# The last expert of a layer: its context rounds, its two scatters and where their row numbers come from

## What is computed

```python
def ec_moe(h, w_router, w_gate, w_up, w_down):
    cap = EC_CAPACITY * length // N_EXPERTS
    aff = jax.nn.softmax((h @ w_router).astype(jnp.float32), axis=-1)
    g, idx = lax.top_k(jnp.swapaxes(aff, 1, 2), cap)
    xg = jax.vmap(lambda hb, ib: hb[ib])(h, idx)
    hid = jax.nn.silu(jnp.einsum('becd,edf->becf', xg, w_gate)) * jnp.einsum('becd,edf->becf', xg, w_up)
    out = jnp.einsum('becf,efd->becd', hid, w_down) * g.astype(h.dtype)[..., None]
    return jax.vmap(lambda ib, ob: jnp.zeros((length, dim), ob.dtype).at[ib.reshape(-1)].add(ob.reshape(-1, dim)))(idx, out)
...
x_lat = x_lat + mod[5] * ec_moe(h_lat, ...)
if not last:
    x_ctx = x_ctx + mod_c[5] * ec_moe(h_ctx, ...)
```

## Time and profile before

| | |
|---|---|
| time, median of three runs | 2590.0 us (2586.6 to 2592.71) |
| span of the profiled execution | 2588.7 us |
| TensorE busy | 2371.9 us (92%) |
| VectorE busy | 1783.0 us (69%) |
| ScalarE busy | 1378.9 us (53%) |
| GpSimd busy | 204.1 us (8%) |
| experts of layer 0, from the first gather to the last scatter's landing | 746.5 to 1529.6 us |
| experts of layer 1, likewise | 1978.7 to 2563.9 us |

### The profile page before, as it was taken

One profiled execution on the slowest core, in us unless ns is written; L12 is line 12 of the kernel. 1 busy time (PEld: TensorE's weight loads), 2 busy tenths in 40 slices (PEclk: granted clock), 3 DMA queues, 4 the chain that ended last, 5 costly groups with the idle time before them and its releaser, 6 DMA issues.

```text
span 2588.7 us, 34812 instructions
## 1 busy us (share of the span) xinstructions
PE 2371.9 (92%) x13396; PEld 1831.0 (71%) x13396; DVE 1783.0 (69%) x1997; ACT 1378.9 (53%) x1410; POOL 204.1 (8%) x220
## 2 busy tenths in 40 slices
PE   6999999989849999999999969988984999999994
PEld 4887777678636666666666647876864788888883
DVE  6523213455587888888888767566658899999995
ACT  6310113334525666656666644657353777777774
POOL 0000000000010211111111010000000011111110
PEclk9999999999879999999999988999997999999997
DMA  6034545735316887887887851112355999999995
GB/s 246 25 105 133 166 143 124 291 116 212 139 51 259 292 302 291 292 303 282 297 307 277 308 176 29 29 37 77 123 183 190 351 377 398 390 388 387 387 378 187
DMA packets 194343, 585.58 MB, mean 226 GB/s; under 512 B 19656, under 2 KB 64448, under 8 KB 187712
## 3 DMA queue, kind: packets, MB, share of 16 engines
q1 hardware_dynamic: 178688, 529.61, 54.9%
q0 software_dynamic: 12336, 48.24, 7.2%
q10 hardware_dynamic: 3216, 6.29, 0.7%
HBM read 536.88 MB, written 47.21 MB: 226 GB/s over the span
## 4 chain that ended last, share of the span: by engine, by line
PE 85%; DVE 6%; DMA 4%; ACT 4%; issue 1%; SPq 0%; POOL 0%; POOLq 0%; ACTq 0%; DVEq 0%
PE ps L1662 14%; PE ps L1664 13%; PE ps L1663 13%; PE ps L1677 7%; PE ps L578 5%; PE ps L579 4%; PE ps L580 4%; PE ps L849 3%; PE ps L850 3%; PE ps L851 3%; PE ps L515 1%; PE ps L549 1%; PE ps L615 1%; DMA R_W<-in_ada_w 1%; PE ps L617 1%
## 5 line engine op out<-in xcount | busy, mean ns | idle before, releaser
L1888 DVE TENSOR_TENSOR R_H_r<-R_M,R_W_r 128x2048 fp32r<-128x2048 f32 x336 | 759.0, 2287 | 141.0 <-ACT R_W_r L1790 138.6
L1790 ACT CAST R_W_r<-R_M 128x2048 fp32r<-128x2048 f32 x336 | 640.0, 1915 | 214.9 <-PE ps L1664 213.6
L1664 PE MATMUL ps<-R_W_r,R_C_r 128*128 128x512 f32 x1536 | 606.0, 395 | 0.0
L1662 PE MATMUL ps<-R_W_r,bc_r 128*128 128x512 f32 x1024 | 411.6, 402 | 5.8 <-ACT R_W_r L1790 2.9
L1663 PE MATMUL ps<-R_H_r,bc_r 128*128 128x512 f32 x1024 | 403.3, 394 | 0.0
L1664 PEld LDWEIGHTS ps<-R_W_r,R_C_r 128*128 128x128 f32 x1536 | 288.6, 188 | 65.6
L1662 PEld LDWEIGHTS ps<-R_W_r,bc_r 128*128 128x128 f32 x1024 | 192.5, 188 | 65.3 <-issue 10.9
L578 PE MATMUL ps<-R_H_r,R_W_r 128*128 128x512 f32 (+1 forms) x632 | 232.7, 368 | 4.9 <-ACT R_W L2251 2.0
L579 PE MATMUL ps<-R_C_r,R_W_r 128*128 128x512 f32 (+1 forms) x632 | 229.4, 363 | 0.0
L580 PE MATMUL ps<-R_H_r,R_W_r 128*128 128x512 f32 (+1 forms) x632 | 228.9, 362 | 0.0
L1663 PEld LDWEIGHTS ps<-R_H_r,bc_r 128*128 128x128 f32 x1024 | 192.5, 188 | 42.2
(11 more groups left out here) (323 smaller groups left out, 3766.3 us busy)
## 6 DMA issues: line engine op xcount, KB each, us to landing
R_M<-in_moe_w_gate SPq DMA_DIRECT2D x114, 1024.0 KB, 8.3
R_M<-in_moe_w_down SPq DMA_DIRECT2D x112, 1024.0 KB, 9.3
R_M<-in_moe_w_up SPq DMA_DIRECT2D x110, 1024.0 KB, 7.8
bc<-in_ada_w SPq DMA_DIRECT2D x28, 1024.0 KB, 4.9
R_H<-in_moe_w_up SPq DMA_DIRECT2D x18, 1024.0 KB
R_H<-in_moe_w_down SPq DMA_DIRECT2D x16, 1024.0 KB
R_H<-in_moe_w_gate SPq DMA_DIRECT2D x14, 1024.0 KB
R_W<-in_ev_w_in SPq DMA_DIRECT2D x25, 512.0 KB, 3.9
```

Source lines behind the costliest of these rows:

```text
L1662: pe.matmul(o, hi[:, k, :], wh[:, kk, cs], start=(k == 0), stop=False)
L1664: ins = pe.matmul(o, lo[:, k, 0:P], wh[:, kk, cs], start=False, stop=(k == KC - 1))
L1790: nc.scalar.copy(whi[j], raw[slot + j]).then_inc(unit_high_done, 1)
L1888: nc.vector.tensor_tensor(wlo[j], raw[slot + j], whi[j], ALU.subtract).then_inc(unit_low_done, 1)
```

## The change

On TensorE the context rounds of expert 15, with their two waits, are put ahead of its four units; a wait for the hidden rows goes with them, and the loads are waited for inside. On VectorE the context result goes ahead of the latents'. On POOL the last scatter of a layer has a function of its own: the context rows first, then the latents', with the row numbers read from the table, without the copies. In layer 1, where `C` is 0, only the copy of the latents' row numbers goes, and POOL's waits change their order.

```diff
             moe_steps(pe, step)
-            pe.wait_ge(expert_rows_done, n0 + NE - 1)
-            down(NE - 1, NE // 2 - 1, 1)
             if C:
                 pe.wait_ge(context_down_half_copied, n0 + NE - 1)
                 pe.wait_ge(context_down_summed, n0 + NE - 1)
-                context_matrix(2, NE - 1, NE // 2 - 1, 1, hctx[1], 6)
+                pe.wait_ge(hidden_low_done, n0 + NE)
+                context_matrix(2, NE - 1, NE // 2 - 1, 1, hctx[1], 6, ahead=True)
+            pe.wait_ge(expert_rows_done, n0 + NE - 1)
+            down(NE - 1, NE // 2 - 1, 1)
...
             low(2, NE - 1, NE // 2 - 1, 1, 3)
-            result(NE - 1)
             if C:
                 context_result(NE - 1, 6)
+            result(NE - 1)
...
+            def scatter_last():
+                count, n, e = n0 + NE, n0 + NE - 1, NE - 1
+                pool.wait_ge(rows_scattered, n * 16)
+                if C:
+                    pool.wait_ge(context_rows_scattered, n * 16)
+                    pool.wait_ge(context_expert_rows_done, count)
+                    pool.indirect_dma_start(out=xres, out_offset=bass.IndirectOffsetOnAxis(ap=icolT[0:C, e + 32:e + 33], axis=0),
+                                            in_=outc[0:C, :], in_offset=None, compute_op=ALU.add).then_inc(context_rows_scattered, 16)
+                    pool.sem_inc(context_scatter_index_set, 1)
+                pool.wait_ge(expert_rows_done, count)
+                pool.indirect_dma_start(out=xres, out_offset=bass.IndirectOffsetOnAxis(ap=icolT[:, e:e + 1], axis=0),
+                                        in_=eout, in_offset=None, compute_op=ALU.add).then_inc(rows_scattered, 16)
+                pool.sem_inc(scatter_index_set, 1)
...
             scatter(n0 + NE - 1, False)
-            scatter(n0 + NE, False)
+            scatter_last()
```

## The result

The changed kernel takes **2594.1 us** (median of 18 runs, 2591.1 to 2595.9), the kernel before, in runs taken beside them, 2588.9 us (18 runs, 2581.9 to 2593.8). The ratio is 1.0018, with a 95% interval of 1.0011 to 1.0025: 5.1 us slower, where 5.2 were forecast. It is on the edge that the prediction named: 0.18%, beside the 0.2% that it took for the least that can be told from no change. With 18 runs the interval, 2.8 to 6.5 us, lies wholly on the slower side.

A forecast was written before the change was run, and what follows sets the result against it. TensorE and what hangs behind it was taken to bound the kernel. Layer 0's latents landing 5.45 us later, less 0.21 us at layer 1's end, gave +5.2 us on the 2590.0 us median: 2595.2 us, range 2589.5 to 2598.5.

The forecast's parts named there:

- the first case of the prediction: Whole kernel: clock falls in the new idle, latents land in 8.2 us as before; +5.2 us, chance 0.43.
- The idle: End of layer 0: TensorE waits 2.8 us for VectorE's two adds before expert 15's context rounds.
- The clock: TensorE's clock falls to 1.2 GHz after the new idle, costing 1.5 us, between bounds of nothing and 1.5.
- The rival that the clock holds: TensorE's clock stays at 2.4 GHz through the idle: +3.7 us, 2593.7 us in all, chance 0.25.
- The units: Expert 15's four units on TensorE take 11.4 us instead of 12.15, the wait for the low part gone.
- The direct row numbers: Latents' last scatter without the copy of its row numbers starts 0.21 us sooner after VectorE, in either layer.
- The landing: Latents' last scatter in layer 0 lands in 8.2 us as before, from below 6.2, from above 10.4.
- The context rows: Expert 15's context scatter leaves GpSimd by 1524.4, ahead of the latents' at 1526.82: hidden, 2.4 us of cover.
- The weight loads: Layer 1's three loads start at 1524.7 and land by 1532.9: hidden, with 5 us for the splits.
- the old slack of 1.5 us: End of layer 0 before the change: latents landed at 1528.03, context rows at 1529.57; context rows alone win 1.5 us at most.
- an earlier clock in layer 1: Layer 1's first stage: clock returns sooner, up to 5.7 us less, -0.5 us in all, 2589.5 us; chance 0.10.

The follow-up runs named there:

- e1_bank7: Changed kernel with expert 15's context rounds in bank 7, without the two waits for bank 6: stage 28.99 us, ratio 1.0006 to the kernel before.
- e6_busy11: Changed kernel with 11 filler matmul calls on TensorE ahead of the two waits: stage 31.12 us, ratio 1.0009 to the kernel before.
- e4_early: Changed kernel with layer 1's three weight loads issued up to three units earlier: stage 31.23 us, ratio 1.0017 to the kernel before.
- e3_copies: Changed kernel with the copies of the row numbers back ahead of both last scatters: stage 33.10 us, one run.
- e9_table_alone: Kernel before with only the last scatters' row numbers taken from the table, latents first: stage 27.83 us, ratio 0.9996 to the kernel before.
- e5_both: Changed kernel with both bank 7 for expert 15's context rounds and the early weight loads: stage 26.72 us, ratio 0.9994 to the kernel before.
- e7_latents_first: e5_both with the latents' result and scatter ahead of the context's on VectorE and GpSimd: stage 27.89 us, ratio 0.9994 to the kernel before.
- e8_own_buffer: e5_both with expert 15's context product in the buffer of the gathered context rows: stage 26.61 us, ratio 0.9991 to the kernel before.
- e10_old_order_early: e9_table_alone with layer 1's three weight loads issued up to three units earlier: stage 28.89 us, ratio 1.0003 to the kernel before.
- e11_own_again: The kernel of e8_own_buffer measured once more: stage 26.74 us, ratio 0.9992 to the kernel before.
- e12_splits_behind: e8_own_buffer with VectorE's weight splits waiting for a count behind GpSimd's latents' scatter: stage 27.20 us, ratio 0.9991 to the kernel before.

## Why the prediction was right

The time, the sign and the path came out, and nearly every term. The 0.18% lie within the 0.2% that had a chance of 0.56; the first case of the prediction, clock falls and landing as before, is the one that came (0.43).

- **The idle**: 2.8 us forecast, 2.74 measured; VectorE's adds end at 1510.94 and PE starts at 1511.05. e1_bank7 shows that the bank is its cause.
- **The clock**: taken at 1.5 us between bounds of 0 and 1.5, measured 1.69 by the rounds and 1.75 by e6_busy11. The upper bound itself was 0.2 too low; it was worked out from other matmuls. The rival that the clock holds (0.25) is out for this idle. The Trainium skill (TensorE: Matmul & The Clock Gate, section HAM oscillation) names only gaps longer than this as the danger; the traces disagree: in three executions of three the clock fell behind 2.74 us (0.50 granted in the changed kernel's stretch behind it, 0.55 in e4_early's, 0.54 in e3_copies').
- **The units**: 11.4 us without the wait for the third unit's low part; 11.32 measured (1516.31 to 1527.63).
- **The direct row numbers**: 0.21 us in each layer. This is the term that was mis-sized: in layer 0 it is 0.72 (1.00 to 0.28), in layer 1 0.25 (1.00 to 0.75). The step took the context scatter's 0.79 us as the price of a scatter whose numbers are ready. e9_table_alone shows that the same context scatter, with its numbers from the table, starts after 0.28.
- **The landing**: 8.2 us taken from the earlier trace rows, 8.3 measured. So close a match is luck in part: with the three loads beside, the seven traces that have them lie between 7.8 (e3_copies) and 9.1 us (e1_bank7). Without the loads it is 5.9 to 7.3 us (e4_early, e5_both, e7_latents_first, e8_own_buffer, e10_old_order_early, e11_own_again, e12_splits_behind).
- **The context rows**: hidden, as said. Their product waits for expert 14's scatter (landed 1520.03, product 1520.12), GpSimd is through at 1523.51, and the latents' scatter begins 5.7 us later, more cover than the 2.4 forecast, because the record took 1.33 us and not 4.83.
- **The weight loads**: hidden, with less to spare than forecast. The last landed at 1538.13, 10.5 us after the loads began at 1527.63, where 8.2 were allowed; the third split on ScalarE began at 1538.15, the first work on the stream at 1540.81. That is 2.7 us of cover, where 5 were forecast.

Sum of the stage: the old slack of 1.5 us (latents landed 1528.03, context rows 1529.57) comes off, and 2.74 + 3.57 + 1.69 - 0.83 (units 12.15 to 11.32) - 0.72 = 6.45 are added, with 0.1 for the landing: 5.05 against 5.06 measured and 5.45 forecast. With 0.25 from layer 1 that is 4.8, beside 5.1 in the medians. The forecast of 5.2 came closer than its terms: the clock's fall was taken 0.2 too small and the saving of the row numbers 0.5 too small, and the two errors work against each other. In the time alone, with an interval of 2.8 to 6.5 us, the hit within 0.1 us is luck; what bears the account out are the terms of the stage.

The rival of **an earlier clock in layer 1** can't be ruled out for one execution: in the changed kernel's profile the 17 us that answer to those of the earlier trace rows, 7.9 us later as the stage is, had 0.75 granted where before had 0.50, and layer 1 was 2.5 us shorter there. This row is that stretch (columns as in rows 11):

```profile
1561.10:1578.10 17.00, 11.95 (x50) 9.62 (x49) 12.56 (x24) 13.75 (x23) 0.00 (x0) 0.75 0.00 1
```

But the medians of 18 runs differ by what the stage and layer 1's end differ by, within the interval of some 2 us either way, so on average at most that much of it is left; it would then belong to what one kernel's executions differ by (12 us between the lowest and the highest of the kernel before).

## What to carry to other kernels

A step that is moved to the front of a queue takes its waits along: ask which buffer it writes and who reads that one last, and give it one of its own before anything else. Before moving the last of two parallel ends, read how far the second is behind: here 1.5 us, and everything that pushed the second back was paid in full beyond that. A transfer that starts with the last instruction of a stage lies beside the scatter that ends it, and made its landing 2.4 us longer here: start it some units earlier, where the scatter that it lies beside is the last one. Then look at what its arrival sets going: here VectorE's splits came forward and lay under the start of that scatter.

## What was not expected of the hardware

- **Landing of a scatter has two parts.** With no loads beside, the context rows (32 rows) landed 2.2 us after the end of GpSimd's record (1.33 + 2.2 = 3.5 to 4.83 + 2.2 = 7.0 us; with loads, up to 4.1, as in e4_early, where it is 5.4 - 1.33), and the latents' (128 rows) 4.4 to 4.8 us after it with no loads beside, 6.2 to 7.5 us with the three.
- **The record's length goes by what VectorE does when it begins.** The fourteen traces have 672 scatters. Of these, 369 begin while none of VectorE's low splits runs (TENSOR_TENSOR, L1888 and L974 of the kernel before): their records last 1.33 to 1.38 us (context) or 1.55 to 1.62 us (latents), also where a split begins after them. The other 303 begin while a split runs, and all but one are longer: 1.56 to 4.83 us and 2.29 to 3.64 us. The one, the latents' of e5_both, lasted 1.56 us. Where a record begins while one of the three splits for layer 1 runs, it ends just behind a split, wherever it began:

| scatter | begins after the first split's start, us | record, us | ends after the end of |
|---|---|---|---|
| context, before | 0.86 | 1.56 | the second, by 0.07 |
| context, e9_table_alone | 0.35 | 2.07 | the second, by 0.08 |
| context, e7_latents_first | 0.83 | 2.72 | the third, by 0.08 |
| context, e10_old_order_early | 0.35 | 3.21 | the third, by 0.07 |
| latents, e5_both | 1.09 | 1.56 | the second, by 0.30 |
| latents, e4_early, e8_own_buffer, e11_own_again | 0.36 | 2.29 | the second, by 0.30 |
| latents, e12_splits_behind | 0.18 | 2.47 | the second, by 0.30 |

So the splits hold the record up, as far as traces side by side can show it: in the changed kernel, where the loads come late, they begin after the latents' record, and it is 1.56 us. No run moved the splits alone, as e12_splits_behind was meant to do, and why it is now the second and now the third split stays open. The Trainium skill (SBUF — State Buffer, section Who interferes with whom) says that a VectorE instruction with two SBUF inputs contends with a GpSimd instruction that reads SBUF; these records would fit. Holding the splits back until the scatter has landed was not run.

- **A semaphore count behind an indirect scatter can come before its record.** In e12_splits_behind VectorE was let go by 1526.33, the record runs from 1526.51 to 1528.98 (one execution; the profile's spans on GpSimd are rough), and the rows landed at 1533.80. Such a count doesn't tell that the scatter is written.
- **How soon a scatter starts after VectorE's end** takes three values: 1.0 us with a copy of row numbers, 0.75 to 0.79 as the first scatter with numbers from the table, 0.28 as the second (after, e8_own_buffer, e9_table_alone, e10_old_order_early). e7_latents_first is the exception, a second scatter at 0.76 whose data were ready 0.28 us after the first one's record ended. What decides it wasn't found.
